# A decoder trunk on one Trainium2 core: half of the 48 wide conditioning-weight transfers of the prelude are issued from ScalarE's queue

## What is computed

```python
cond = jax.nn.silu(c)
for i in range(DEPTH):                       # DEPTH = 2
    mod = jnp.einsum('bd,sdk->bsk', cond, ada_w[i]) + ada_b[i]
    shift_t, scale_t, gate_t = jnp.split(mod[:, 0], 3, axis=-1)
    shift_m, scale_m, gate_m = jnp.split(mod[:, 1], 3, axis=-1)
    h = modulate(rmsnorm(x, norm_g[i, 0]), shift_t, scale_t)
    y = pool_mixer(h, ...) if i % 2 == 0 else retention(h, ...)
    x = x + gate_t[:, None, :] * y
    h = modulate(rmsnorm(x, norm_g[i, 1]), shift_m, scale_m)
    x = x + gate_m[:, None, :] * sq_relu_mlp(h, mlp_w1[i], mlp_w2[i])
return rmsnorm(x, final_g)
```

## Time and profile before

| | us |
|---|---|
| time, median of 3 | 2337.06 |
| lowest and highest | 2336.86, 2339.1 |
| span of the profiled execution | 2336.1 |
| PE busy | 2251.9 |
| DVE busy | 1681.1 |
| ACT busy | 1084.2 |
| HBM traffic over the span | 284 GB/s |

### The profile page before, as it was taken

One profiled execution on the slowest core, in us unless ns is written; L12 is line 12 of the kernel. 1 busy time (PEld: TensorE's weight loads), 2 busy tenths in 40 slices (PEclk: granted clock), 3 DMA queues, 4 the chain that ended last, 5 costly groups with the idle time before them and its releaser, 6 DMA issues.

```text
span 2336.1 us, 28515 instructions
## 1 busy us (share of the span) xinstructions
PE 2251.9 (96%) x10033; PEld 1817.7 (78%) x10033; DVE 1681.1 (72%) x1814; ACT 1084.2 (46%) x1342; POOL 139.9 (6%) x249
## 2 busy tenths in 40 slices
PE   4489999999999999999999999999999999999998
PEld 2147788888888887888888888887888888888887
DVE  4668889788887898777676767677877555555557
ACT  2324554544544545444454444555553453453454
POOL 0000000100100100001000001000100000000000
PEclk9689999999999999999999999999999999999999
DMA  9999989998998977888766887876997776776774
GB/s 400 415 413 393 339 297 328 364 367 277 368 334 292 362 281 231 303 264 275 246 233 215 299 260 244 273 239 202 333 359 248 235 230 195 226 232 191 232 228 152
DMA packets 276674, 664.21 MB, mean 284 GB/s; under 512 B 21768, under 2 KB 22200, under 8 KB 269632
## 3 DMA queue, kind: packets, MB, share of 16 engines
q1 hardware_dynamic: 260320, 611.92, 75.8%
q0 software_dynamic: 15328, 49.87, 6.2%
q10 hardware_dynamic: 896, 0.75, 0.1%
HBM read 638.30 MB, written 24.14 MB: 284 GB/s over the span
## 4 chain that ended last, share of the span: by engine, by line
PE 88%; DMA 2%; DVE 2%; ACT 1%; issue 0%; POOLq 0%; POOL 0%; SPq 0%; DVEq 0%; ACTq 0%
PE acc L701 86%; DMA raw<-in_mlp_w 2%; PE acc L1122 1%; DVE w_lo L1601 1%; PE score_ps L1109 0%; ACT w_hi L1173 0%; DVE ada_acc L1607 0%; PE score_ps L908 0%; PE tb L848 0%; DVE ev L1903 0%; PE tb L983 0%; DVE x L1907 0%; DVE scratch L1773 0%; DVE scratch L1768 0%; PE mod_ps L856 0%
## 5 line engine op out<-in xcount | busy, mean ns | idle before, releaser
L1601 DVE TENSOR_TENSOR w_lo<-raw,w_hi 128x1024 fp32r<-128x1024 f32 x775 | 943.3, 1223 | 558.6 <-ACT w_hi L1173 555.5
L1173 ACT ACTIVATE w_hi<-raw 128x1024 fp32r<-128x1024 f32 x775 | 821.8, 1061 | 1094.8 <-PE acc L701 971.5
L701 PE MATMUL acc<-w_hi,h_lo 128*128 128x512 f32 x1788 | 698.5, 391 | 2.6 <-issue 1.6
L701 PE MATMUL acc<-w_hi,h_hi 128*128 128x512 f32 x1788 | 695.8, 389 | 0.0
L701 PE MATMUL acc<-w_lo,h_hi 128*128 128x512 f32 x1788 | 695.8, 389 | 0.0
L701 PE MATMUL acc<-w_hi,a_lo 128*128 128x512 f32 x1308 | 511.6, 391 | 0.4 <-DVE w_lo L1601 0.4
L701 PE MATMUL acc<-w_lo,a_hi 128*128 128x512 f32 x1308 | 510.3, 390 | 0.0
L701 PE MATMUL acc<-w_hi,a_hi 128*128 128x512 f32 x1308 | 510.0, 390 | 0.0
L701 PEld LDWEIGHTS acc<-w_hi,h_lo 128*128 128x128 f32 x1788 | 335.7, 188 | 75.1 <-issue 4.1
L701 PEld LDWEIGHTS acc<-w_hi,h_hi 128*128 128x128 f32 x1788 | 335.7, 188 | 70.0
L701 PEld LDWEIGHTS acc<-w_lo,h_hi 128*128 128x128 f32 x1788 | 335.8, 188 | 68.5
(11 more groups left out here) (216 smaller groups left out, 912.9 us busy)
## 6 DMA issues: line engine op xcount, KB each, us to landing
raw<-in_mlp_w SPq DMA_DIRECT2D x512, 512.0 KB, 5.1
ada_raw<-in_ada_w SPq DMA_DIRECT2D x248, 512.0 KB, 6.6
raw<-in_ret_w_in SPq DMA_DIRECT2D x192, 512.0 KB, 4.6
ada_early_h<-in_ada_w SPq DMA_DIRECT2D x32, 1024.0 KB, 13.4
raw<-in_ret_w_out SPq DMA_DIRECT2D x64, 512.0 KB, 4.4
ada_raw<-in_ada_w SPq DMA_DIRECT2D x16, 1024.0 KB, 12.5
square_blocks<-ev POOLq DMA_DIRECT2D x112, 128.0 KB, 4.8
ev<-square_blocks POOLq DMA_DIRECT2D x28, 512.0 KB, 6.4
```

Source lines behind the costliest of these rows:

```text
L701: mm = nc.tensor.matmul(acc[pair][t][:], l[:, CK * c + j, tok], w[:, slot, j, :], start=first and j == 0 and i == 0, stop=last and j == CK ...
L1173: nc.scalar.activation(w_hi[:, o % RING], raw[:, o % RING], ACT.Copy).then_inc(hi_ready, 1)
L1601: nc.vector.tensor_tensor(w_lo[:, o % RING], raw[:, o % RING], w_hi[:, o % RING].bitcast(F32), ALU.subtract).then_inc(lo_ready, 1)
```

## The change

Of the 48 wide pieces SP issues the 24 even ones; the 24 odd ones are issued from ACT's queue, at places in ACT's program that are written out by hand. The slots, the semaphores, the users and the sizes stay as they are, and so do the programs of PE, DVE and POOL. In the diff `load_odd(seg, w)` issues piece w of segment seg.

```diff
@@ SP: load_early
                 wide = seg < WIDE_SEGS
-                if wide and a % 2:
+                if wide and a % 4:
                     return
@@ ACT
+            def load_odd(seg, w):
+                g = seg * SEG + 2 * w
+                if g >= EARLY:
+                    if ON_PE[g - EARLY]:
+                        act.wait_ge(ada_pe, PE_BEFORE[g - EARLY + 1] + 1)
+                    else:
+                        act.wait_ge(ada_done, DVE_BEFORE[g - EARLY + 1] + 1)
+                slot, to = wide_slot(seg, 2 * w)
+                act.dma_start(to, ada_rows[0, w * P:(w + 1) * P, seg, :]).then_inc(ada_in[slot], 16)
+
             act.dma_start(rows[0:KT, 1, :], c_in...).then_inc(cond_in, 16)
             act.dma_start(ident[:], ident_in).then_inc(const_in, 16)
+            for w in (1, 3, 5):
+                load_odd(0, w)
             act.wait_ge(cond_in, 16)
...
             for b in range(4):
                 squares(b)
+            for w in (7, 9):
+                load_odd(0, w)
...
             nc.scalar.activation(norm_band_1, band_1, ACT.Copy, scale=rstd[:, 1:2]).then_inc(band_ready, 1)
+            for w in (11, 13, 15):
+                load_odd(0, w)
             for f in range(KT // 2):
                 first_norm(f)
+                if f in (1, 3, 5):
+                    load_odd(1, f)
             n.add(TB=CH)
             copy_rows(mod_ps, 1, PE_BEFORE[SEG])
+            for w in (7, 9, 11, 13, 15):
+                load_odd(1, w)
+            for w in (1, 3):
+                load_odd(2, w)
             copy_rows(score_ps, 1, PE_BEFORE[2 * SEG])
```

More of the change, by code:

```diff
@@ L1294, in first_gate @@
                 n.add(RM=1, GB=4)
+            ada_rows = ada_w.rearrange("i s d (j k) -> (i s) d j k", j=3)
+            def load_odd(seg, w):
[7 more added lines that the diff above has]
+                act.dma_start(to, ada_rows[0, w * P:(w + 1) * P, seg, :]).then_inc(ada_in[slot], 16)
             gate_bias = ada_b.rearrange("i s (j k) -> (i s j) k", j=3)[2]
@@ L1352, in _ @@
             hi(1)
+            load_odd(2, 5)
             modulated(1)
             pooled_hi(0)
+            load_odd(2, 7)
             modulated(2)
@@ L1358, in _ @@
             hi(3)
+            load_odd(2, 9)
             modulated(3)
@@ L1361, in _ @@
             pooled_hi(3)
+            load_odd(2, 11)
             hi(4)
@@ L1364, in _ @@
             evacuate_group(0)
+            load_odd(2, 13)
             hi(6)
@@ L1367, in _ @@
             evacuate_group(1)
+            load_odd(2, 15)
             first_gate()
```

## The result

| | before | after |
|---|---|---|
| median of 5 runs each (us) | 2337.4 | 2348.32 |
| lowest and highest | 2336.86, 2339.1 | 2345.34, 2348.52 |
| span of the profiled execution | 2336.1 | 2346.5 |

The ratio is 1.004, with a 95% interval from 1.0028 to 1.0051. Times 2337 that is 9.4 us slower, with an interval from 6.5 to 11.9: twice what was forecast. Ratios and intervals leave out one far slower execution each of e2 (5896.51 us), b3 (2562.84) and b6 (3759.58), which the medians of the table of experiments still count.

The account below looks back on a forecast made before the run. The prediction took the prelude up to W47 to be bound by DMA bytes. Its terms, 4.2 us at the start and 0.6 at segment 2's end, summed to +4.8: 2341.9 us, with an 8-in-10 range of 2335.0 to 2348.0.

Parts of the forecast that it names:

- The bound: Prelude up to W47: bound by bytes, so idle DMA engines before W46 and W47 land delay everything behind.
- rcount: Start: rcount lands about 23.5 us behind 3 MB on ACT's queue, W6 goes out late, engines idle: +4.2 us.
- SP's saving and ACT's issues: Issue time: SP's 24 fewer issues save nothing; ACT's 24 added ones cost zero, at most 2.4 us.
- From 41 to 141 us: Rest of the prelude: even pieces ahead, both queues at half rate, never both empty; cost zero.
- ACT's waits (hi(4)): Mixer: ACT waits for PE's W37 ahead of hi(4), a 2.4 us delay within 5.7 us of slack; cost zero.
- The end of segment 2: W47 up to 2.5 us later, W46 earlier: between -1.3 and +2.5 us, taken as +0.6.
- The checks that it named: Traces: first fill about 51, ACT's row of segment 1 at 98 to 100, row sum of segment 2 near 146.
- the sign that the prediction had named for being wrong: End of segment 2: W47 landing late while the DMA engines were full all along would disprove the forecast.
- Much slower: Rival: ACT starves the transfers, two or three holes add 5 to 8 us, 2346 to 2350; chance 0.15.
- Nothing moves: Rival: rcount lands by 20 us and W6 goes out before 27, 2337 to 2339; chance 0.20.
- Faster: Rival: two queues keep the DMA engines fuller than one, 2333 to 2336; chance 0.10.

Follow-up runs that it names:

- e2: Changed kernel, but only segment 0's odd pieces issued from ACT, rcount still behind W1, W3 and W5: 2343.57 us, ratio 1.0021.
- b3: Changed kernel, but only segment 0's odd pieces issued from ACT, with rcount issued ahead of them: 2337.52 us, ratio 1.0.
- b6: Changed kernel with rcount ahead of the odd pieces and, on SP, pool_w chunks 6 and 7 moved behind W40 and W42: 2339.68 us, ratio 1.001.
- e4: Kernel before, all wide pieces on SP, with rcount issued late, behind ACT's wait for x: 2343.94 us, ratio 1.0025.
- e1: Changed kernel, all odd pieces on ACT, with rcount issued right behind ident, ahead of W1, W3 and W5: 2341.36 us, ratio 1.0015.
- b1: Kernel before, SP issuing all wide pieces, with the changed kernel's 24 waits added on ACT: 2338.41 us, ratio 1.0004.
- b2: Changed kernel, but only segment 2's odd pieces issued from ACT, segments 0 and 1 all on SP: 2341.93 us, ratio 1.0017.
- e3: Changed kernel, but only the odd pieces of segments 1 and 2 issued from ACT, segment 0 all on SP: 2341.74 us, ratio 1.0018.
- c4: Changed kernel with rcount first, pool_w chunks 0 to 3 between W20 and W26, chunks 6 and 7 behind W40 and W42: 2346.52 us, ratio 1.0037.
- c1: b2 with each of ACT's odd pieces split by columns into four transfers, rows of 2 KB: 2345.61 us, ratio 1.0032.
- c2: b2 with each of ACT's odd pieces split by columns into two transfers, rows of 4 KB: 2342.18 us, ratio 1.0015.

## Why the prediction was right in part

**The bound, right.** Whatever idles the DMA engines before 141 us delays all behind it: e4 shows it one for one, 5.8 us for 5.8, and the lag of 9.4 at the row sum is 9.5 at L742.

**rcount, right in place and nearly in size.** Forecast 23.5 for DVE's start, measured 24.47; W6 30.1 against 30.93; 345 GB/s and a share of 0.8 against 317 and 0.83; 4.2 us against 5.0. The rule of the Trainium skill (DMA: Bandwidth & Descriptors, section Queues, rings and completion order) that a ring is served in order agrees with this trace: the same 32 KB take 7.4 us with nothing large ahead of them on their queue, 9.8 ahead of W1 in e1, and 18.0 behind 3 MB. The engines ran short from 28 us on, as forecast. ACT did have half of the engines (51.1 and 50.3%).

**SP's saving and ACT's issues, right.** Both at zero. b3, which moves eight issues from SP to ACT and stays level, shows it for segment 0; b1 shows it for the waits ahead of ACT's issues.

**"From 41 to 141 us": the step that failed.** The prediction took the even pieces to be ahead of the odd ones, let both run at half rate, and said that "this costs bytes only if a moment comes at which both queues are empty". No such moment came, the share is 1.00 or more until 140 us, and bytes were not what it cost. Its count of SP's hold was near (W30 out at 85, measured 86.57). But it counted two queues of equal pieces, though the chunks of pool_w stand in SP's queue alone. At 87 us SP had 2 MB of chunks ahead of W32 and ACT had none, so W33 and W35 were in before W32. The prediction did look at ACT's waits (hi(4)) and at W47, and not at the chain that starts with a late even piece: DVE's low halves, SP's holds at chunks 4 and 6, W40. It put this stretch at zero; eight pieces of it cost 4.0 us in b2.

**"The end of segment 2", mis-sized.** It had +0.6, from an order in which W47 is late and W46 early. It was the reverse: W47 was in, W46 was last. b2, e1 and e3 put the part beyond rcount at 3.5 to 4.2 us. With 4.0 in the place of 0.6 and 5.0 in that of 4.2 the prediction's sum is +9.0, and +9.4 was measured. That is a sum put right afterwards, with a term that was measured in another kernel (b2).

**The checks that it named.** The first fill came at 53.25 (forecast 51), ACT's row of segment 1 at 101.86 (98 to 100), the row sum at 150.44 (146). They are 2.3, 1.9 to 3.9 and 4.4 us later than forecast, where the start was late by 1, and with a full share in between: the sign that the prediction had named for being wrong ("landed late while the DMA engines were full all along"), with the even pieces in the place of W47.

**The rivals.** "Much slower" has the measured time (2346 to 2350) but not the mechanism: it wanted holes of ACT's making beyond 60 us, and there are none. c4 has such a hole, made on SP's side. "Nothing moves" is b3: right for segment 0 if rcount goes first. b3 also agrees with the rule of the Trainium skill cited there (DMA: Bandwidth & Descriptors, section Issuing engines are not separate DMA queues), that all issuers end on the same 16 engines; e1 and b2 pay for the order, which is another matter. "Faster" is nowhere: with both queues full the stretches show 412 to 419 GB/s, with SP alone 411 to 422. The median of 2348.32 is 0.3 above the range's upper end; the ratio puts the time at 2346.4, inside it. The range is not quite what its own words give: the middle of the faster rival is 2334.5, and the much slower one starts at 2346 by its heading and at 2347 by its text. By them the measured time stands at the edge; that the range as stated holds it owes nothing to the mechanism. The start of the first data is also stated twice, at 2.4 us and at 2.6; the 0.2 us changes nothing.

**Open.** That the order in which the bytes arrive makes the second part was followed step by step in b2, and b6 undoes a part of it by order alone. What was not run is the harmful order on one queue: SP issuing everything, with W33 and W35 ahead of the chunks and W32. It would part the order from anything else that a second queue does. Of the 4 us, W32's 5.1 us and SP's hold are counted off in b2. How much of the 3.1 us that W40 loses on its way (16.3 us instead of 13.2) is the size of the rows and how much is ACT's two pieces beside it was not taken apart; c1 gives 2 us of it back but delays the odd pieces.

The 3.1 us at b2's row sum are 3.1 at L742 as well, and its span is 4.4 longer. Most of the last 1.3 us lies near 900 us, in a part of the program that no edit touches. From 900 to 950 us the granted clock of PE is 0.97 in the profiles of b2, e3, e4 and the changed kernel, so for a part of it the clock was at the lower of its two levels (1.2 instead of 2.4 GHz), though PE is busy for 48 us or more of the 50. The kernel before, e1, b1, c1 and c2 have 1.00 there. Across it (L833, 894.1 and 902.1 us in the kernel before) b2's lag grows from 2.8 to 3.9 us and the changed kernel's from 8.8 to 10.1. The five timed runs of the changed kernel go the same way: the two with a granted clock of 0.990 and 0.989 over the span took 2345.34 and 2346.1 us, the three with 0.982 to 0.984 took 2348.3 to 2348.5. Whether the shift in time brings the lower clock was not tested. So a microsecond or so of these losses may be the clock's and not the transfers'.

In the stretches from 140 to 180 us the share of the changed kernel is 0.97 where it was 1.02 to 1.03: SP starts segment 3 at 143.30 instead of 130.15 because DVE frees the slots late. It did not add to the lag at L742.

## What to carry to other kernels

Here, with the DMA engines full, one queue in order of need was a schedule; a second queue gave nothing and took the schedule away. Before adding a queue, count for each piece the bytes that are now ahead of it, in both queues, and follow the late one through whoever waits for it. A share of 1.0 says that bytes flow, not that the right ones do. A small load on which a chain hangs goes ahead of large ones on its queue; in a stretch bound by bytes, time in which the engines are idle is time of the total (e4: 5.8 us for 5.8).

## What was not expected of the hardware

- Two queues with 8 KB rows shared the DMA engines evenly (51.1 and 50.3%), and with 2 KB rows on one side the division was 28.1 to 73.4%. Yet halving or quartering the rows of the favoured side (c1, c2) did not bring the other side's next piece forward, though c1's favoured side had 16.2% of the engines from 81.9 to 90 us where b2's had 30.5.
- The same 1 MB took 8.6 us to landing on one queue and 19.9 on the other, issued in the same 15 us (b2), with the engines full.
- In c1 rows of 2 KB moved 400 to 406 GB/s at a share of 1.03 to 1.04, rows of 8 KB 412 to 416 at 1.02: a full share is not one rate.
- Issuing a transfer is not always short. SP's issue of W32, right behind four chunks with 2 KB rows, took 4.30 us before and 7.72 in b2, where most issues of a wide piece take 0.33. It need not cost anything here, since SP then stood 10 us and more at chunk 4 in both.
